# Sample values from one packed operand in two passes, and a second-half step ahead of a late first-half step

## What is computed

```python
h = rmsnorm(x) * (1 + scale) + shift
# layer 0, four groups of 512 channels
u, z = split(h @ w_in);  y = (pool_mix(u) * silu(z)) @ w_out
# layer 1, four heads
q, k, v, z, gl = split(h @ w_in);  y = (norm(gla(q, k, v, decay(gl))) * silu(z)) @ w_out
x = x + gate * y
```

## Time and profile before

| | us |
|---|---|
| median of 3 runs | 1639.38 |
| lowest and highest | 1637.96, 1642.22 |
| the profiled execution, its own time | 1641.13 |
| its span, first to last instruction | 1638.7 |
| PE busy | 1601.3 |
| DVE, ACT, POOL busy | 819.3, 446.9, 356.3 |

### The profile page before, as it was taken

The page is one execution under the profiler, slowest core; times in us unless marked ns, Lnnn a source line. Parts: engine busy times, 40 slices in busy tenths (PEclk is TensorE's granted clock), DMA queues, the critical chain, the costliest instruction groups (busy, mean ns, idle before and its releaser), DMA issues.

```text
span 1638.7 us, 24702 instructions
## 1 busy us (share of the span) xinstructions
PE 1601.3 (98%) x9699; PEld 1487.4 (91%) x9699; DVE 819.3 (50%) x1239; ACT 446.9 (27%) x905; POOL 356.3 (22%) x320
## 2 busy tenths in 40 slices
PE   6999999999999999998999999999999999999996
PEld 4899999999999999998888899888997989978896
DVE  4653549343854476447424562245622456224565
ACT  4321112110211021124415404054140442214423
POOL 3021212221121122111303213032230321303210
PEclk8999999999999999998999999999999999999998
DMA  9612221221122112210202212022120221201302
GB/s 323 204 56 78 68 64 47 75 72 53 55 72 72 55 56 68 78 41 28 64 14 65 91 47 73 8 68 91 44 73 14 65 97 40 66 25 40 116 32 109
DMA packets 137544, 115.01 MB, mean 70 GB/s; under 512 B 6013, under 2 KB 120281, under 8 KB 137442
## 3 DMA queue, kind: packets, MB, share of 16 engines
q1 hardware_dynamic: 135616, 112.87, 22.4%
q10 hardware_dynamic: 1834, 0.74, 0.2%
HBM read 99.05 MB, written 15.00 MB: 70 GB/s over the span
## 4 chain that ended last, share of the span: by engine, by line
PE 94%; DVE 3%; SPq 1%; DMA 1%; ACT 1%; issue 0%; ACTq 0%; DVEq 0%
PE psA L550 40%; PE psB L550 29%; PE psB L1804 8%; PE psA L1804 4%; PE psB L1860 2%; PE psB L1877 2%; PE psB L1868 2%; PE psX L1897 1%; DVE a_hi L638 1%; PE psX L1842 1%; PE psB L1909 1%; PE psX L1720 1%; DMA ada<-in_ada_w 1%; DVE y_rows L1606 0%; PE psB L1910 0%; PE psX L1661 0%
## 5 line engine op out<-in xcount | busy, mean ns | idle before, releaser
L345 POOL TENSOR_TENSOR w_lo<-stage,w_hi 128x1024 fp32r<-128x1024 f32 x100 | 249.7, 2497 | 904.1 <-ACT w_hi L340 904.0
L340 ACT ACTIVATE w_hi<-stage 128x1024 fp32r<-128x1024 f32 x100 | 106.9, 1069 | 435.9 <-PE psB L550 297.5
L550 PE MATMUL psA<-h_hi,w_hi 128*128 128x362 f32 (+1 forms) x864 | 210.8, 349 | 4.0 <-DVE h_lo L454 3.8
L550 PE MATMUL psA<-h_lo,w_hi 128*128 128x362 f32 (+1 forms) x864 | 193.7, 329 | 0.0
L550 PE MATMUL psA<-h_hi,w_lo 128*128 128x362 f32 (+1 forms) x864 | 193.2, 329 | 0.0
L550 PEld LDWEIGHTS psA<-h_hi,w_hi 128*128 128x128 f32 x864 | 151.4, 190 | 27.1 <-issue 21.2
L550 PEld LDWEIGHTS psA<-h_lo,w_hi 128*128 128x128 f32 x864 | 151.5, 190 | 0.0
L550 PEld LDWEIGHTS psA<-h_hi,w_lo 128*128 128x128 f32 x864 | 151.4, 190 | 0.0
L550 PE MATMUL psA<-a_hi,w_hi 128*128 128x362 f32 (+1 forms) x480 | 109.6, 334 | 2.5 <-DVE a_lo L641 2.5
L550 PE MATMUL psB<-h_hi,w_hi 128*128 128x362 f32 (+1 forms) x480 | 109.7, 331 | 0.0
L550 PE MATMUL psB<-h_hi,w_lo 128*128 128x362 f32 (+1 forms) x480 | 107.9, 327 | 0.0
(11 more groups left out here) (344 smaller groups left out, 2692.0 us busy)
## 6 DMA issues: line engine op xcount, KB each, us to landing
stage<-in_gla_w_in SPq DMA_DIRECT2D x40, 512.0 KB, 3.8
stage<-in_pool_w_in SPq DMA_DIRECT2D x32, 512.0 KB, 4.1
ada_stage<-in_ada_w SPq DMA_DIRECT2D x24, 512.0 KB, 3.8
ada<-in_ada_w SPq DMA_DIRECT2D x16, 512.0 KB, 8.3
stage<-in_pool_w_out SPq DMA_DIRECT2D x16, 512.0 KB, 3.4
v<-in_state_gla SPq DMA_DIRECT2D x32, 256.0 KB, 2.6
out_new_gla_sample<-v SPq DMA_DIRECT2D x32, 256.0 KB, 2.1
stage<-in_gla_w_out SPq DMA_DIRECT2D x16, 512.0 KB, 3.6
```

Of the source, the lines that this page charges most:

```text
L340: nc.scalar.activation(slot_hi(plan, j), stage[:, j % 2, :], ACT.Copy).then_inc(lay.hi_done, 1)
L345: nc.gpsimd.tensor_tensor(slot_lo(plan, j), stage[:, j % 2, :], slot_hi(plan, j).bitcast(f32), ALU.subtract).then_inc(lay.lo_done, 1)
L550: last = nc.tensor.matmul(ps[u][:, t, 0:width], weight(w[:, p, :], k), a[:, k, n0:n0 + width], start=(k == 0 and pas == 0), stop=(k == kt ...
```

## The change

The sample columns of `h_hi` and `h_lo` are copied side by side into `hs_both` (64 columns high, 64 low) at the start of each head, behind the end of Q. The ninth value block then takes two matmuls for each contraction step (packed by high weights, packed by low weights) in place of three; PSUM rows 0 to 63 get the product of the high parts, rows 64 to 127 that of the low parts. DVE adds the two halves, counts the evacuation up, and makes `v_s` from the sum in SBUF. In `project_inner` with parts (O01 of each pool group), step 0 of the second half is issued between step 2 and step 3 of the first half.

```diff
+        hs_both = sb("hs_both", [P, KD, 2 * NS], f32r, stack=values)
...
+        v_part, v_sum = G[0:NS, 0:GW], G[0:NS, GW:2 * GW]
...
         def project_inner(pe, lay, plan, g, name, ready, parts=None):
+            p, c = plan.slot[name] % 2, plan.set[plan.unit[name]]
+            if parts:
+                set_ready(pe, lay, plan, g, plan.unit[name])
+                slot_ready(pe, lay, plan, g, name)
+                for k in range(KG - 1):
+                    pe.wait_ge(ready, g * KG + k + 1)
+                    product_step(p, c, k, KG, w4(0), a_hi, a_lo)
+                set_ready(pe, lay, plan, g, plan.unit[name] + 1)
+                product_step(p, plan.set[plan.unit[name] + 1], 0, KG, w4(1), a_hi, a_lo)
+                for t in range(3):
+                    pe.wait_ge(parts, g * 3 + t + 1)
+                    last = product_step(p, c, KG - 1, KG, w4(0), a_hi, a_lo, (t,))
+                last.then_inc(lay.unit_done, 1)
+                for k in range(1, KG):
+                    last = product_step(p, plan.set[plan.unit[name] + 1], k, KG, w4(1), a_hi, a_lo)
+                last.then_inc(lay.unit_done, 1)
+                return
...
+                dve.wait_ge(L1.unit_done, units(GP, g, GP.unit["Q"] + 1))
+                nc.vector.tensor_copy(hs_both[:, :, 0:NS], h_hi[:, :, TP:T])
+                nc.vector.tensor_copy(hs_both[:, :, NS:2 * NS], h_lo[:, :, TP:T]).then_inc(hs_both_ready, 1)
                 dve.wait_ge(sp_ready, g + 1)
...
-                            link(nc.vector.tensor_copy(v_s[0:NS, :], src[0:NS, j, :]))
-                            last = nc.vector.tensor_tensor(v_s[NS:P, :], src[0:NS, j, :], v_s[0:NS, :].bitcast(f32),
-                                                           ALU.subtract)
+                            link(nc.vector.tensor_copy(v_part, src[NS:P, j, :]))
+                            last = nc.vector.tensor_tensor(v_sum, src[0:NS, j, :], v_part, ALU.add)
                     last.then_inc(L1.evac[GP.set[u]], 1)
+                    if i == 2:
+                        dve.wait_ge(L1.evac[GP.set[u]], evacs(GP, g, u))
+                        link(nc.vector.tensor_copy(v_s[0:NS, :], v_sum))
+                        nc.vector.tensor_tensor(v_s[NS:P, :], v_sum, v_s[0:NS, :].bitcast(f32),
+                                                ALU.subtract).then_inc(vs_ready, 1)
...
+                            if s == NSUP:
+                                if k == 0:
+                                    pe.wait_ge(hs_both_ready, g + 1)
+                                for pas, w in enumerate((wv_hi, wv_lo)):
+                                    last = nc.tensor.matmul(ps[GP.set[u]][:, j, :], hs_both[:, k, :], w[k // 2][:, c],
+                                                            start=(k == 0 and pas == 0), stop=(k == KD - 1 and pas == 1))
+                                continue
...
                 def sample_update(b):
+                    if b == 0:
+                        pe.wait_ge(vs_ready, g + 1)
```

More of the change, by code:

```diff
@@ L192, in trunk @@
         att_lo = sb("att_lo", [P, NS], f32r, stack=heads)
+        values = ExitStack()
+        sb("values_before", [P, NSUP - 2, GW], stack=values)
+        hs_both = sb("hs_both", [P, KD, 2 * NS], f32r, stack=values)
+        values.close()
         v = sb("v", [P, NSUP, GW], stack=heads)
@@ L297, in trunk @@
         s0_ready, smp_upd = sem("s0_ready"), sem("smp_upd")
+        hs_both_ready, vs_ready = sem("hs_both_ready"), sem("vs_ready")
         S_stored = sem("S_stored")
@@ L589, in project_inner @@
                     slot_ready(pe, lay, plan, g, name)
[L590 to L599, removed]
+                c = plan.set[u]
                 product(pe, p, c, KG, w4(half), a_hi, a_lo,
@@ L1801, in value_rows @@
                             s = 3 * i + j
+                            if s == NSUP:
[5 more added lines that the diff above has]
+                                continue
                             for pas, (h, w) in enumerate(((h_hi, wv_hi), (h_lo, wv_hi), (h_hi, wv_lo))):
-                                n = P if s < NSUP else NS
-                                last = nc.tensor.matmul(ps[GP.set[u]][0:n, j, :], h[:, k, s * P:s * P + n],
+                                last = nc.tensor.matmul(ps[GP.set[u]][:, j, :], h[:, k, s * P:(s + 1) * P],
                                                         w[k // 2][:, c],
```

## The result

| | before | after |
|---|---|---|
| median, us (4 runs each) | 1640.80 | 1628.13 |
| lowest to highest | 1637.96 to 1642.60 | 1627.03 to 1629.99 |
| ratio, 95% interval | | 0.9928 (0.991 to 0.9946) |
| profiled execution, its own time | 1641.13 | 1629.99 |
| its span | 1638.7 | 1628.3 |

The forecast was 1628, between 1624.5 and 1632.5. It started from the median of three runs of the kernel before, 1639.38 us; the fourth, 1642.60, moved that median to 1640.80. The kernel became 0.7% faster; in microseconds the interval of the ratio spans 8.9 to 14.8.

What follows compares the result with a forecast made beforehand. PE, busy 98% of the span, was taken as the bound; 7.35 us from the removed passes plus 4.38 us from the order in O01 gave 11.73, so 1639.38 became 1627.65, predicted as 1628, range 1624.5 to 1632.5.

Steps and rivals of the forecast that it cites:

- PE's list is the time: Whole kernel: PE, busy 98% of the span, sets the time; a removed matmul is worth its spacing to the next.
- The passes removed: VC of each head: 8 matmuls fewer at 0.2296 us each, 1.84 us a head, 7.35 us over four heads.
- The rival of half the price: Sample passes in VC: packed passes give nothing or half, being slower or the removed ones having overlapped; chance 0.05.
- The copies at the head's start cost nothing: Behind the end of Q: two DVE copies of 128 x 512 fit in DVE's idle time; cost nothing.
- DVE's chain behind VC is hidden with 0.7 us to spare: Behind VC: added cast and subtract end the products at about 5.2 us, PE asks at 5.89; cost nothing.
- The new PE waits cost nothing: Three new PE waits a head find their semaphores already counted up: taken as nothing, upper end 2.8 us.
- The order in O01: O01 of four pool groups: moving step 0 of the second half ahead removes 1.095 us a group, 4.38 us.
- The span's sum: Whole kernel: 7.35 + 4.38 = 11.73 us less, the span going from 1638.7 to 1627.0 us.

Runs made afterwards that it cites:

- second edit alone: Kernel before with only step 0 of O01's second half moved ahead of the first half's last step, sample values in three passes: 1635.82 us, ratio 0.9978.
- split late: Kernel before, old order and three passes, with ACT's weight split behind Z3 waiting until the last a_lo part is made: 1636.39 us, ratio 0.9977.
- first edit alone: Changed kernel with packed sample values but the old order in O01, against the kernel before: 1631.38 us, ratio 0.9952.
- the two runs with the cover cut: Three steps of Z0 instead of four ahead of the sample scores: in the changed kernel 1632.23 us, in the kernel before 1640.38 us.
- two steps ahead: Changed kernel with steps 0 and 1 of O01's second half ahead of the first half's last step: 1628.47 us, ratio to before 0.9931.

## Why the prediction was right

- *PE's list is the time.* Right. The first edit shortens PE's list, the second takes a wait out of it, and the time followed: 7.7 and 3.3 us alone, 11.0 and 12.7 us together in the two measurements, 11.73 forecast. That the median came within 0.2 us of the forecast 1628 is luck: its four runs spread over 3 us, and the median that the forecast started from moved by 1.4 us.
- *The passes removed.* Right; the term was 7.35 us, the four heads of the profile gave 6.95, the medians 7.7. VC lost 1.75 us in the second head where 1.84 was worked out. The step "a packed pass costs the same 0.2296 us" holds: from start to start, the 24 sample passes of this unit took 5.50 us before (0.229 each) and the 16 packed ones take 3.68 (0.230 each), 1.82 us less. The rest lies in the full blocks, which the edit does not change: their 48 matmuls took 11.03 us and take 11.10. Nor do the 0.4 us that four heads lack say that the term was too large: three profiles of kernels with three passes and the cover whole (before, second edit alone, split late) differ by 0.7 us from the first VA to the last output unit (806.80 to 807.49).
- *The rival of half the price.* Not borne out. At 0.166 us a matmul the heads would have given 5.3 us, under the 6.95 of the profile and just under the interval of the first edit alone (5.7 to 9.8 us). In medians it would have meant about 1630 (1639.38 less 4.38 for the order, 1635.0, less 5.3), and 1635.0 with nothing from the passes; the median was 1628.13.
- *The copies at the head's start cost nothing.* Right: 0.43 and 0.42 us in a gap that was 28 us long; 0.43 is also what was allowed for a cast of this width when it is not held.
- *DVE's chain behind VC is hidden with 0.7 us to spare.* Right to 0.1 us: the last product ends 5.09 us behind VC, forecast 5.2, PE asks at 5.87. The cast was held as worked out, and ended 0.28 us behind POOL's split (up to 0.43 allowed). The two runs with the cover cut show that the reserve is real and that it is small: a quarter of `fill(4)` less and each head waits.
- *The new PE waits cost nothing.* Right as far as the profile shows: no gap at the packed block, and none in the first half of O01.
- *The order in O01.* Right: 1.095 us a group forecast, 1.10 found, and the stretch of the groups is 4.45 us shorter in every profile with this order and one or two steps ahead (4.38 forecast); the whole first half with the moved step 7.56 us forecast, 7.55 found. That it would be more than the 0.65 us of PE's own wait row was the point. The weight loads' list comes close, 4.7 us in eight waits: the second part was late as well, and behind both late parts the first matmul's weight load starts with the matmul and not ahead of it (both at 181.49, both at 182.89); the matmul then takes 0.43 us and not 0.33, and the next starts 0.27 us later and not 0.165.
- *The span's sum.* 11.73 us forecast, 10.4 in the profiled pair. The 1.3 us lacking are 0.4 us of the passes, and 1.48 us between the layers, less 0.55 us at the kernel's start; neither stretch is touched by the edits, and both differ from run to run: from the start to the first long unit it is 99.46 to 101.74 us in the ten profiles, between the layers 51.99 to 53.74.

## What to carry to other kernels

On an engine that is busy from end to end, price a removed instruction by the start-to-start spacing in its own stream (here 0.23 us, where a row of the trace is 0.39 long) and check two things: what the other engines must finish before the shorter list comes to its next wait, and how much time they have to spare there. A stationary operand that fills half the array cost a whole pass here (0.23 us with 64 columns as with 128), so two half-filled operands side by side save one. Where an operand comes late, read the waits of the weight loads beside those of the matmuls, and look for other work of the same engine that is ready and doesn't disturb the order of releases; one step was enough here, two did no harm, a third met the next release. And ask why it is late: here another engine's instruction held DVE up (a cast took 2.58 us beside it, 0.35 without), and moving that one was worth as much (4.45 us of the groups' stretch either way).

## What the hardware showed unexpectedly

Between the layers, where neither edit has a part, PE adds up squares by 54 matmuls with one moving column, back to back. The two windows below are of the same program, first in the run shown above and then in its repetition; the row is stretch, length, busy time of PE, PEld, DVE, ACT and POOL, granted clock, DMA share, GB/s. PE was busy for 8.80 of 8.80 us in the first and 7.65 of 7.70 in the second.

```profile
742.73:751.53 8.80, 8.80 (x55) 8.64 (x54) 1.80 (x5) 3.36 (x5) 2.35 (x1) 0.67 0.00 0
```

```profile
744.20:751.90 7.70, 7.65 (x55) 7.49 (x53) 1.80 (x5) 3.33 (x6) 2.34 (x1) 0.78 0.00 0
```

The same stretch in the kernel before:

```profile
747.73:754.89 7.16, 7.15 (x55) 6.99 (x54) 1.80 (x5) 3.37 (x5) 2.35 (x1) 0.85 0.00 0
```

The mean clock of the stretch is 0.67, 0.78 and 0.85 of full, and its length goes with it: length times mean clock is 5.9, 6.0 and 6.1 us. The granted clock falls from 1.00 (737 to 742, the products of the last group) to 0.50 (747 to 751) in the first of these runs while PE is still issuing these sums; it is 1.00 up to 745, in the repetition up to 748 and in the kernel before up to 752. In the chains of all ten profiles the 54 sums take 7.00 (before) to 8.86 us (the second edit alone), and the same program gave 8.65 and 7.55. So 1.1 us of difference between two profiles of one program, and up to 1.9 us between two of these ten (mean clock in the sums 0.84 and 0.64), go with the point of this stretch at which the clock falls, and not with an edit; a span read from one profile is uncertain by that much. Why it falls earlier in one run than in another was not tried.
